# Gathering tile 0's rows while tiles 1 to 3 are ranked, in a two-block network on one core

## The reference

```python
def peer_ffn(xn, w_q, keys1, keys2, u_tab, v_tab):
    q = (xt @ w_q).reshape(T, PEER_HEADS, 2, PEER_HALF)
    s1 = jnp.einsum('thd,kd->thk', q[:, :, 0], keys1)
    s2 = jnp.einsum('thd,kd->thk', q[:, :, 1], keys2)
    v1, i1 = lax.top_k(s1, PEER_TOPK)            # 16 of 128
    v2, i2 = lax.top_k(s2, PEER_TOPK)
    cand = (v1[..., :, None] + v2[..., None, :]).reshape(...)
    cidx = (i1[..., :, None] * PEER_KEYS + i2[..., None, :]).reshape(...)
    top, pos = lax.top_k(cand, PEER_TOPK)        # 16 of 256
    eidx = jnp.take_along_axis(cidx, pos, axis=-1)
    g = jax.nn.softmax(top, axis=-1)
    # per chunk of tokens, with u_tab and v_tab of 16384 rows by 1024
    a = jax.nn.gelu(jnp.einsum('td,thkd->thk', xc, u_tab[ec]))
    return jnp.einsum('thk,thkd->td', gc * a, v_tab[ec])
```

## Time and profile before

| | us |
|---|---|
| median of 3 runs (3501.59 to 3506.4) | 3506.13 |
| the profiled execution, its own time | 3473.59 |
| its span | 3471.6 |
| busy in the span: PE, DVE, POOL, ACT | 3083.6, 1598.3, 766.3, 509.9 |
| ranking stage, from the last queries to the first instruction of the memory stage | 2102.4 to 2265.2 |
| coefficient pass, from there to the first `weigh` | to 2382.0 |
| first quarter, to the first `weigh` of the second | to 2587.6 |
| second and third quarter | to 3143.7 |
| fourth quarter, to the last v add | to 3379.0 |

### The profile page before, as it was taken

One profiled execution on the slowest core, in us unless ns is written; L12 is line 12 of the kernel. 1 busy time (PEld: TensorE's weight loads), 2 busy tenths in 40 slices (PEclk: granted clock), 3 DMA queues, 4 the chain that ended last, 5 costly groups with the idle time before them and its releaser, 6 DMA issues. The chain is left out here.

```text
span 3471.6 us, 35875 instructions
## 1 busy us (share of the span) xinstructions
PE 3083.6 (89%) x11536; PEld 1821.1 (52%) x11536; DVE 1598.3 (46%) x3312; ACT 509.9 (15%) x1071; POOL 766.3 (22%) x688
## 2 busy tenths in 40 slices
PE   8998799989987589877889889689999999999986
PEld 1444644446434323323447568587567777776553
DVE  0123500103011312121234329988998878887772
ACT  2122310001101011122125321100000000000002
POOL 0000000000000011110000001155766556556650
PEclk9899899999998699988989999857999999999998
DMA  7201012120123888751300024257999999999992
GB/s 304 99 25 50 1 49 90 62 82 13 73 97 143 327 338 323 314 227 54 117 13 1 1 80 133 86 186 243 352 368 390 362 363 363 364 362 371 410 364 103
DMA packets 156221, 668.47 MB, mean 193 GB/s; under 512 B 22115, under 2 KB 31587, under 8 KB 140771
## 3 DMA queue, kind: packets, MB, share of 16 engines
q1 hardware_dynamic: 73540, 383.09, 29.0%
q0 software_dynamic: 81792, 281.07, 21.6%
q10 hardware_dynamic: 800, 3.15, 0.2%
HBM read 689.25 MB, written 35.65 MB: 209 GB/s over the span
## 5 line engine op out<-in xcount | busy, mean ns | idle before, releaser
L2262 PE MATMUL ps<-wring,pm_weighted 128*128 128x512 f32 x1024 | 474.6, 607 | 34.0 <-DVE pm_weighted L2364 33.9
L346 PE MATMUL ps<-hT,wring 128*128 128x512 f32 (+2 forms) x1232 | 468.8, 543 | 16.3 <-PEq L505 4.9
L2236 POOL DMA_INDIRECT pm_ring<-in_peer_u,pm_idxs x256 | 329.5, 1287 | 172.2 <-DVE pm_dots L2377 89.4
L346 PEld LDWEIGHTS ps<-hT,wring 128*128 128x128 f32 (+1 forms) x1232 | 235.9, 192 | 246.1 <-issue 237.3
L2245 PE MATMUL ps<-hT,wring 128*128 128x256 f32 x1536 | 352.7, 383 | 0.5 <-DMA wring<-in_peer_v 0.5
L2431 DVE SCALAR_TENSOR_TENSOR pm_acc<-pm_ring,pm_coefs,pm_acc 128x1024 f32<-128x1024 f32 x256 | 317.7, 1283 | 59.6 <-DMA pm_ring<-in_peer_v,pm_idxs 59.0
L2236 POOL DMA_INDIRECT pm_ring<-in_peer_v,pm_idxs x256 | 297.9, 1164 | 143.6 <-DVE pm_acc L2431 59.8
L2254 PEld LDWEIGHTS ps<-pm_onehot,hT 128*128 128x128 f32 x2048 | 293.1, 225 | 49.4 <-issue 48.3
L2262 PEld LDWEIGHTS ps<-wring,pm_weighted 128*128 128x128 f32 x1024 | 192.8, 193 | 240.1 <-issue 188.8
L2245 PEld LDWEIGHTS ps<-hT,wring 128*128 128x128 f32 x1536 | 286.8, 190 | 50.0 <-issue 14.4
L1304 POOL COPY ex_idx<-row_token 128x1 uint32 (+1 forms) x24 | 4.4, 184 | 1349.9 <-PEq L1417 1157.8
(11 more groups left out here) (418 smaller groups left out, 3256.6 us busy)
## 6 DMA issues: line engine op xcount, KB each, us to landing
ex_gu<-in_experts SPq DMA_DIRECT2D x48, 2048.0 KB
wring<-in_peer_v SPq DMA_DIRECT2D x128, 512.0 KB, 7.1
ex_dn<-in_experts SPq DMA_DIRECT2D x48, 1024.0 KB
wring<-in_peer_uT SPq DMA_DIRECT2D x96, 512.0 KB, 5.7
wring<-in_w_in SPq DMA_DIRECT2D x21, 2048.0 KB, 7.8
wring<-in_w_ada SPq DMA_DIRECT2D x12, 2048.0 KB, 7.8
pk_u<-in_peer_uT SPq DMA_DIRECT2D x32, 512.0 KB, 3.8
y_dram_out<-gates SPq DMA_DIRECT2D x1, 12288.0 KB, 32.3
```

The lines of the kernel that those rows point to most:

```text
L346: mm = env.nc.tensor.matmul(out, w[:, k, lo:hi], rhs(k), start=(k == 0), stop=(k == KD - 1))
L2236: nc.gpsimd.indirect_dma_start(ring[:, r, :], None, dram[table], bass.IndirectOffsetOnAxis(ap=idx[:, half, r:r + 1], axis=0)).then_inc(got ...
L2262: mm = nc.tensor.matmul(env.ps[:, OUT[n], :], W[:, s % 2, t * P:(t + 1) * P], vr[s][:, half * WBLK:(half + 1) * WBLK], start=False, stop=stop)
```

## The change

The scores of 96 dense blocks instead of 32 are made in the ranking stage (three quarters, `AHEAD`, `FIRST` = 96), with a first run of 8 blocks ahead of tile 2's key scores, then 28, then 60. The coefficients' side stays where it was. POOL no longer does a number product; from tile 0's row numbers on it issues the 128 u gathers of tile 0 in the ranking stage. DVE does both number products, and between the issue of each group of tiles 1 to 3 and the wait for it two dots (`FILL`) are placed, 128 in all. In the memory stage 384 gathers remain. Its order on DVE becomes: 32 `one_hot` alone; first quarter with 96 v adds of tile 0 (3 a block); second with 32 v adds (2 a block, 16 blocks) and 48 u dots of tile 1 (3 a block, 16 blocks); third with 80 u dots (2 or 3 a block); fourth with 128 v adds as before. Three quarters read their score tiles back from DRAM, with the wait for the `outputs` of two blocks earlier.

```diff
-MIDDLE = PB * 5 // 8
-EARLY = PB
-LATE = (SLOTS - EARLY) * RING // PB
+AHEAD = PARTS - 1
+FIRST = AHEAD * PB
+TABLE = (8, 36, 66)
+FILL = 2
@@ Group.__call__ @@
+    def __call__(self, eng, steps, then=None):
         for ins in steps:
             ins.then_inc(self.sem, 1)
             self.env.chained += 1
+        if then is not None:
+            for _ in range(FILL):
+                then()
         eng.wait_ge(self.sem, self.env.chained)
@@ ranking stage, POOL @@
-                for t in range(NT):
-                    pool.wait_ge(place_s, t + 1)
-                    number(nc.gpsimd, 1).then_inc(match_s, 1)
+                pool.wait_ge(rows_s, 1)
+                for n in range(SLOTS):
+                    if n >= RING:
+                        pool.wait_ge(G.used, n - RING + 1)
+                    nc.gpsimd.indirect_dma_start(G.ring[:, n % RING, :], None, dram["peer_u"], ...)
@@ ranking stage, ACT @@
                 queries(1)
+                table(0, TABLE[0])
                 exponentials(0)
                 key_scores(2)
-                table(0, MIDDLE // 2)
+                table(TABLE[0], TABLE[1])
                 exponentials(1)
-                table(MIDDLE // 2, MIDDLE)
                 key_scores(3)
+                table(TABLE[1], TABLE[2])
                 exponentials(2)
-                table(MIDDLE, PB)
+                table(TABLE[2], FIRST)
                 exponentials(3)
@@ ranking stage, DVE @@
+                def dot():
+                    n = next(dots)
+                    if n < SLOTS:
+                        ve.wait_ge(G.got[n % RING], ...)
+                        V.tensor_tensor_reduce(G.ring[:, n % RING, :], ..., xg[:, 0, :], ...,
+                                               G.coef[:, n:n + 1]).then_inc(G.used, 1)
-                    match(1).then_inc(place_s, 1)
-                    group(ve, [match(0)])
-                    group(ve, [number(V, 0)])
-                    ve.wait_ge(match_s, t + 1)
+                    group(ve, [match(a) for a in range(2)])
+                    group(ve, [number(a) for a in range(2)])
+                        if t == 0:
+                            ve.sem_inc(rows_s, 1)
+                            gathering = True
@@ memory stage, SP @@
-                with sp.Fori(0, TURNS) as i:
+                with sp.Fori(0, AHEAD * TURNS) as i:
                     for s in range(STEP):
                         m = STEP * i + s
                         sp.wait_ge(out_done, STEP - 1 + m)
...
@@ memory stage, PE @@
-                scores(TURNS, 0)
-                for part in range(1, PARTS - 1):
+                for part in range(AHEAD):
                     with pe.Fori(0, TURNS) as i:
                         for s in range(STEP):
-                            scores(*after(part * TURNS + i, s))
                             outputs(part * TURNS + i, s)
                             coefficients(part + 1, i, s)
+                scores(AHEAD * TURNS, 0)
@@ memory stage, DVE @@
+                coefficients(0)
+                with v.Fori(0, TURNS) as i:
+                    for s in range(STEP):
+                        one_hot(0, i, s)
+                v.wait_ge(c_done, 2 + PB)
+                adding(0, 0, TURNS, 2, 12, SLOTS, 0)
+                v.wait_ge(c_done, 2 + 2 * PB)
+                adding(1, 0, TURNS // 2, 2, 8, SLOTS + 96, 96)
+                sums(0, 2 * SLOTS)
+                dotting(1, TURNS // 2, TURNS // 2, 2, 24, 2 * SLOTS, 0, 1)
+                v.wait_ge(c_done, 2 + 3 * PB)
+                dotting(2, 0, TURNS, 4, 40, 2 * SLOTS + 48, 48, 3)
+                coefficients(1)
+                v.wait_ge(c_done, 2 + 4 * PB)
+                adding(3, 0, TURNS, 1, PER, 3 * SLOTS, 0)
+                sums(1, 4 * SLOTS)
```

More of the change, by code:

```diff
@@ L1978, in store @@
                     nc.sync.dma_start(dram["g_dram"][m], g[:, m % STEP, :]).then_inc(g_out[m % STEP], 16)
[L1980 removed]
+                for m in range(FIRST):
                     if m >= STEP:
@@ L1985, in _ @@
                         store(m - STEP)
-                for m in range(PB - STEP, PB):
+                for m in range(FIRST - STEP, FIRST):
                     store(m)
@@ L2148, in _, with stage_memory @@
                 finish(NT - 1)
-def stage_memory(env, rows, pairs, gate, xg):
+                for _ in range(SLOTS):
+                    dot()
+def stage_memory(env, rows, pairs, gate, xg, G):
     nc, dram = env.nc, env.dram
-    assert PB == TURNS * STEP == DS // GRP and PER % STEP == 0 and EARLY // RING + PB // RING == TURNS
-    got, got0 = zip(*(env.again(f"gathered{r}", 16 * 2 * GT * SLOTS // RING) for r in range(RING)))
+    assert PB == TURNS * STEP == DS // GRP
+    got, got0, used, ring, coef = G.got, G.got0, G.used, G.ring, G.coef
     table_got, table0 = [], 0
```

209 lines of the change are left out of this document (98 added, 111 removed).

## The result

The changed kernel takes 3546.99 us (median of 4 runs, 3527.75 to 3556.57), the kernel before 3503.86 (4 runs, 3489.06 to 3506.4): a ratio of 1.0125, 95% interval 1.0074 to 1.0176. It is 43 us slower, not the same, and 39 us above the 3508 forecast. The two rivals of the slower side (the loop of loads; the ranking bound by the DMA) come nearest. The changed kernel's profiled execution took 3548.31 us, with a span of 3546.3.

What follows compares the result with a forecast made beforehand. Three resources take turns as the bound, with PE alone bounding the 556 us the change takes work from. Ranking +184.8 and memory stage -182.5 gave +2.3, 3475.9; with 32.5 us added for the median, 3508; 8-in-10 range 3476 to 3536.

Steps and rivals of the forecast that it cites:

- the loop of loads: Quarters 2 and 3: v loads waiting for outputs two blocks earlier make 48 lighter blocks 6.3 us each; 3540; chance 0.13.
- the ranking bound by the DMA: Ranking stage: gathers and u loads share 16 engines; at 367 GB/s it ends at 2468, total 3528; chance 0.13.
- The sum: Whole kernel: ranking +184.8 us, memory stage -182.5, total +2.3; chance 0.46 of landing within some 15 us.
- pass: Coefficient pass at the memory stage's start: 118 us, PE setting the pace, nothing gained from the 32 dots leaving.
- first half of quarter 2 with its sums: 16 blocks with 2 adds at 5.5 us each, 88 us, then `sums` of about 3.5 us.
- the rest with the pause: Quarter 2's other 16 blocks 98 us, quarter 3 182 us, pause before quarter 4 8.2 us.
- the prediction's own formula: Loop for two blocks in quarters 2 and 3: 0.9 + 6.3 landing + 0.6 weigh + 3.5 outputs = 11.3 us, 5.65 each.
- PE's part: Ranking stage: 96 blocks at 3.46 us and two key score sets of 2.93 us after the last query; end at 2444.
- The DMA's part: Ranking stage: 127 MB from 2118 on at 390 GB/s, 326 us, to 2444, then 6 us for last dots and `finish`.
- I am wrong if: Signs: coefficient pass under 90 us, ranking ending after 2465, or third quarter under 5.3 or over 6.1 us a block.
- floors: Loads land sooner, quarters 2 and 3 run at their engines' sums, ranking ends with PE at 2444; 3475; chance 0.20.
- Full clock: Coefficient pass stays at 2.4 GHz behind busy PE, running at DVE's 1.81 us: 48 us less, 3460; chance 0.08.

Runs made afterwards that it cites:

- e5: Changed kernel with one added 128x512 zero product behind each block's coefficient products in quarters 1 to 3: 3534.67 us, ratio 1.0108.
- e7: Changed kernel with the ranking's 128 gathers reading 64 of 1024 columns: 3529.05 us in one run.
- e4: Changed kernel with one added 128x512 zero product behind each of the 32 coefficient pass steps: 3507.28 and 3533.93 us in the two executions that count.
- e9: Kernel before with four places for pm_weighted and one 128x512 zero product after each coefficient pass step: 3522.21 us, ratio 1.0084.
- e10: Kernel before, four places for pm_weighted, three zero products behind each of the first four coefficient pass steps, one behind the other 28: 3495.61 us, ratio 1.0012.
- e1: Changed kernel with four places for pm_weighted instead of two, so v loads wait for the block four back: 3471.34 us, ratio 0.9922.
- e6: Changed kernel with four places for pm_weighted and one 128x512 zero product behind each coefficient pass step: 3433.82 us, ratio 0.9841.

## Why the prediction was wrong

The sum said +184.8 for the ranking and -182.5 for the memory stage. Measured in the profiles: last query to the ranking's end 362.1 against 162.8 us (+199.3), last query 4.1 later, which differs from execution to execution (table), memory stage to the first weigh of quarter 4 748.6 instead of 878.5 (-129.9): 73.5 together, against 74.7 between the two executions' own times.

*The loop of loads* is the step that failed, 53 us of it: 748.6 against 696. The prediction had the loop, its 11.3 to 12.6 us and the mechanism; it took the loop at its mean and at full clock, 5.5 us a block in the light half of quarter 2 and 5.7 in quarter 3, and gave the rival that was right 0.13. By pieces: quarter 1 213.7 against 198 (+15.7), first half of quarter 2 with its sums 97.6 against 91.5 (+6.1), the rest with the pause 321.9 against 288.2 (+33.7), pass 115.5 against 118 (-2.5). Between the weighs of a stretch lie 6.59, 6.02, 6.77 and 6.36 us (quarter 1, the halves of quarter 2, quarter 3), where it had 6.17, 5.5, 6.1 and 5.7.

The landing is the smaller part of this. Against the 6.3 of the earlier trace rows the DMA summaries of the four stretches (count, size, median us to landing) have:

```profile
wring<-in_peer_v SPq DMA_DIRECT2D x32, 512.0 KB, 7.4
...
wring<-in_peer_v SPq DMA_DIRECT2D x16, 512.0 KB, 6.0
...
wring<-in_peer_v SPq DMA_DIRECT2D x16, 512.0 KB, 7.1
...
wring<-in_peer_v SPq DMA_DIRECT2D x35, 512.0 KB, 6.8
```

Put into the prediction's own formula, (0.9 + landing + 0.6 + 3.5) / 2, these give 6.2, 5.5, 6.05 and 5.9 us a block: the light half's landing was as the prediction had it, and only quarter 3's 5.7 was too low by it. The rest, 0.4 to 0.7 us a block in all four, lies in what the formula leaves out. The 3.5 us of the outputs are those of full clock; in these quarters PE was busy about 4.2 us with them, in e5 3.7 (395.7 us for 753 products and 357.5 for 776, 8 a block), which the formula turns into 0.25 us a block, an estimate. The prediction left the clock out of these quarters. And a bound of 5.65 beside one of 5.2 was treated by the worse mean, though blocks scatter and what a late load costs isn't won back by the next, early one; this last part is argued, not measured.

Why the loads of quarter 1 land later than before (7.4 against 6.3, at 334 and 348 GB/s) no run tells.

*The ranking stage* is the second, 14.5 us: 362.1 against 347.6. PE's part was right (e7: 341.1 against 341.6), DVE's nearly so: the number products take 2.29 us alone, and the last dot starts at 2415.29, near the 2406 that DVE was given. The DMA's part was mis-sized, 21 us instead of 6. The three windows of the stage have a mean of 354 GB/s, under the 390 that the sum used; but the gathers all stand in the first three quarters of the stage, and there (2128 to 2390 in the first fence) it is 407 GB/s, share 1.03. What PE loses there it can't win back in the last 78 us, at its own 3.45 us a block with a DMA share of 0.68. A mean over a stage hides a stretch that is full. The rival for this stage had the right end, 2468, and not the way to it: it was to decide when DVE's last dot passes 2444, and that dot was done by 2417; PE waited for its blocks of u instead.

*The profile's distance to the median* worked the other way. I added 32.5 us, the gap between before's best execution and its median; the changed kernel's profiled execution lay at its median (3548.3 and 3547.0). In own times the forecast was 3475.9, 72 us low; as a median it is 39 low. The timed difference is 26 to 62 us by its interval, that of the profiles from the last query on 68 to 71 (1441.9 less 1373.7 or 1371.2). The rest isn't settled. In the profiles the quarters with the loop scatter (633.1, 628.8 and 623.0 in the changed kernel, e4 and e7), those of before do not (761.7 and 763.0).

Of the three signs under "I am wrong if" two came: the ranking ended at 2468.5, after 2465 (with the last query where before had it, it would be 2464.4, just inside), and quarter 3 ran at 6.36 us a block, over 6.1.

What was right: the ranking ends behind PE, not DVE (the earlier trace rows had DVE; now DVE waits 49.7 us there); the pass stays near half clock and is as long as before, and the 32 dots that leave it bring nothing by themselves; number products at 2.3 us; quarter 4 unchanged (3217.16 to the end 331.2 us, before 329.9). In e9 PE is busy without a gap at 0.50 for 130 us. By the Trainium skill (TensorE: Matmul & The Clock Gate, section What's actually happening) activity releases the clock; the prediction set that aside on the earlier trace rows, and e9 and e10 agree with the rows.

Of the other rivals "floors" gave 3475, and e1 takes 3471, partly by luck: its quarters are the rival's, its ranking is 20 us longer than the rival has it, and the 32.5 us added for the median make up for that. "Full clock" gave 48 us and e6's edit gives 24 in the pass, as the product itself takes 0.95 us a step.

## What to carry to other kernels

When work that hid a chain of latencies is moved out, price the chain, not only the sums of the engines: (landing + release + the work between) over the number of buffers, with the work at the clock that a waiting PE gets. Here a chain of 5.65 us beside 5.2 us of engine work, by their means, wasn't hidden but cost 6.4. Two more places in that chain turned a loss of 43 us into a gain of 24. And add up DMA bytes by the stretch in which they have to move, not by the stage.
